# A state-space scan in three parts, three back halves copied by ScalarE, row slots inside two injections, the lag readout ahead of the scan's wait

## The chip, the core and the metric

The kernel runs on one core of a Trainium2 chip. The core has TensorE (PE; its weight loads are shown as PEld), VectorE (DVE), ScalarE (ACT), GpSimd (POOL), which here issues DMAs, and SyncE (SP), which issues the DMAs that fill a ring of weight slots. The metric is the device time of one execution in microseconds (us), and the number compared is the median of several executions.

## The reference

The kernel computes two transformer-like blocks in float32. The change touches one mixer of the second block, a diagonal state-space model with 64 groups of 16 channels and 64 complex states, run forward and backward over 256 context and 256 image tokens:

```python
def _ssm_direction(u_lat, u_ctx, a_r, a_i, bb_r, bb_i, c_r, c_i, need_ctx_out):
    ...
    hc_r, hc_i = _diag_scan(a_r, a_i, *inject(u_ctx))
    hx_r, hx_i = _diag_scan(a_r, a_i, *inject(u_lat), h0=(hc_r[-1], hc_i[-1]))
    ...
def _ssm_mixer(xn, cn, w_in, ...):
    u_x = xn @ w_in
    u_c = cn @ w_in
    ...
        y_lat = yf_x + yb_x[::-1]
    ...
        y = y.reshape(u.shape).astype(u.dtype) + d_skip * u
        val, gate = jnp.split(jax.nn.gelu(y) @ w_out, 2, axis=-1)
        return val * jax.nn.sigmoid(gate)
```

Beside it a modulation has to be ready for what follows the mixer: `silu(c) @ ada_w + ada_b`, of which three parts of 1024 columns (24 weight slots of 512 KB) are computed here.

## The kernel before

The 512 tokens are cut into 64 chunks of 8 tokens. What the tokens of a chunk give to the state at its end (the injection) comes from prepared matrices, and so do what the states give to the output (the readout) and what the tokens of a chunk give to each other's outputs (the lags, held as `TOEP`). Between them lies a scan over 64 chunk states. It stands in `XS`, 128 partitions (64 forward, 64 backward) by 64 steps by 2 (real, imaginary) by 64 groups.

**TensorE.** `turn_tokens` and `turn_groups` transpose the projected tokens. `inject(q)` (L1441) injects batch q of 8 groups with 16 matmuls of 128x128 weights and 64 columns, into PSUM at `INJ_SUMS[q]`; a float32 matmul shows as two in the profile, so 32 records. Injections 0 to 3 stand between the projection's tiles (L1467), 4 to 7 stand in a row. Then PE takes the modulation rows, `modulation()`: a generator that reads one ring slot per two steps (`row_part`, L756, two matmuls of 32 weight columns and 512 columns, four records a slot), and after eight slots waits for ScalarE's copy of the row (`row_copied`) and turns it (`turn_row`, L764). `fill(rows, 48)` advances it by 48 steps: 22 of its 24 slots and the first two turns. After that PE waits for `scanned`, and reads out (L1499 the lags, L1502 the two parts of the states, 64 and 128 matmuls, 384 records), in two halves e of 32 groups. Two transposes of the output (L1510), the last two slots (`fill(rows, 4)`), and the gated output projection `linear(8, 8, YT, ...)` (L641) follow; `fill(rows, 2)` behind its first tile turns the third row.

**VectorE** copies the back half of each injection (L2821) as it comes, in two copies of 64 partitions by 512, and scans by `within` (7 steps of a chunk of 8), `across` (6 steps) and `inner` (4 blocks), each step four dependent operations (L2780 to L2783). The groups are cut in two: `first`, 16 groups, whose scan lies between the copies, and `rest`, 48 groups, which begins when all eight injections are copied.

**ScalarE** copies the front half of each injection, then the states of the first groups into `HS` (`states`, eight copies), two modulation rows, the states of the rest (the last of them gives `scanned`), the readout's sums, the GELU, and the third row.

**Queues.** SP refills the four-slot ring: the load of slot m is issued when slot m-3 has begun to be read. POOL loads the batches, 1 MB each, behind waits: batches 0 to 7 are injection matrices, 8 to 15 readout matrices. 12, 9 and 10 wait for the seventh injection, 11 for the eighth, 13 for the landing of 11, 14 for the first inner block of `rest` (`states_ready` 5), 15 for the last (`states_ready` 8).

All orders are written out by hand; each engine executes its own list in order.

## Time and profile before

| | us |
|---|---|
| median of three executions | 3953.61 |
| lowest, highest | 3952.71, 3961.68 |
| the profiled execution | 3964.36 |
| its span, first to last instruction | 3962.6 |
| mean granted clock of TensorE in it | 0.982 of full |

The profiled execution is 10.75 us longer than the median. The stage of the change lies between about 2857 and 2972 us of its span. In a timeline a row gives start, duration, engine, line, operation, shapes, and in brackets the idle time before it and what ended it. The clock is 1.00 at 2.4 GHz and 0.50 at 1.2 GHz.

### The profile page before, as it was taken

Reading aid. Unit: us, or ns where it says so; the run is one execution under the profiler, and the core shown is the slowest. Engines: PE = TensorE matmul, PEld = TensorE weight load, DVE = VectorE, ACT = ScalarE, POOL = GpSimd, SP = SyncE. Lnnn points to the kernel's source line nnn. Section 1 sums busy time; section 2 is a strip of 40 time slices with the busy share of each in tenths; the row PEclk is TensorE's granted clock in tenths of the full one; section 3 lists DMA queues with packets and bytes.
Section 4 is the critical chain, followed back from the end, with each engine's and each line's share of the span. In section 5 each row is a group of like instructions: output and inputs, shape, how many; then the busy total and the mean of one; then the engine's idle time right before and its main releaser. Section 6 shows DMA issues by size and latency. Waiting matters only on the chain.

```text
span 3962.6 us, 61384 instructions
## 1 busy us (share of the span) xinstructions
PE 3851.4 (97%) x21346; PEld 3186.8 (80%) x21346; DVE 2844.3 (72%) x5169; ACT 1584.7 (40%) x2439; POOL 88.3 (2%) x101
## 2 busy tenths in 40 slices
PE   8999999999999999999999999999979999999998
PEld 7897799544977888888888888888748888888887
DVE  6432266894888799999897777776553997777776
ACT  5201053231228444444484444444321094444443
POOL 0000000000000000000000000000400000000000
PEclk9999999999999999999999999999969999999999
DMA  5214555475434666666615666666765516666664
GB/s 194 85 44 127 160 186 158 148 233 179 152 116 138 193 194 191 192 194 188 199 59 186 190 188 188 189 187 207 174 214 162 168 55 196 189 187 190 191 187 152
DMA packets 203773, 666.53 MB, mean 168 GB/s; under 512 B 35920, under 2 KB 46176, under 8 KB 202480
## 3 DMA queue, kind: packets, MB, share of 16 engines
q1 hardware_dynamic: 166816, 602.71, 48.6%
q0 software_dynamic: 12496, 52.53, 4.2%
q10 hardware_dynamic: 24320, 9.37, 0.9%
q8 instruction: 92, 1.51, 0.2%
q14 instruction: 49, 0.40, 0.0%
HBM read 637.34 MB, written 26.15 MB: 167 GB/s over the span
## 4 chain that ended last, share of the span: by engine, by line
PE 89%; DVE 8%; DMA 1%; ACT 1%; issue 1%; SPq 0%; DVEq 0%; ACTq 0%
PE psum L1093 27%; PE psum L1079 17%; PE psum L1081 9%; PE psum L641 6%; PE psum L701 5%; PE psum L726 4%; PE psum L1172 4%; PE psum L1267 3%; PE psum L1161 2%; DVE arena L2367 1%; PE psum L1059 1%; DMA ring<-in_w 1%; DVE arena L2368 1%; PE psum L756 1%; PE psum L1138 1%; DVE arena L2369 1%
## 5 line engine op out<-in xcount | busy, mean ns | idle before, releaser
L1093 PE MATMUL psum<-rows_split_odd,coef_split 128*128 128x512 f32 x2400 | 590.5, 396 | 3.6 <-DVE rows_split_odd L2511 3.6
L1093 PE MATMUL psum<-rows_split,coef_split 128*128 128x512 f32 x2208 | 532.1, 390 | 0.3 <-issue 0.3
L2516 DVE TENSOR_REDUCE work<-psum 128x256 f32<-128x512 f32 x360 | 249.0, 692 | 394.3 <-PE psum L1081 393.2
L1093 PEld LDWEIGHTS psum<-rows_split_odd,coef_split 128*128 128x128 f32 x2400 | 437.9, 188 | 104.9 <-issue 6.8
L1079 PE MATMUL psum<-input_split,rows_split 128*128 128x512 f32 x1440 | 514.0, 397 | 1.2 <-DVE rows_split L2511 1.2
L1079 PE MATMUL psum<-input_split,rows_split_odd 128*128 128x512 f32 x1440 | 510.0, 393 | 0.0
L1726 ACT ACTIVATE work<-work 128x256 f32<-128x256 f32 x360 | 150.7, 419 | 876.8 <-DVE work L2516 876.8
L2511 DVE TENSOR_TENSOR rows_split_odd<-ring,rows_split_odd 128x1024 fp32r<-128x1024 f32 x380 | 462.5, 1218 | 8.9 <-ACT rows_split_odd L1528 8.9
L1093 PEld LDWEIGHTS psum<-rows_split,coef_split 128*128 128x128 f32 x2208 | 401.9, 188 | 81.6 <-issue 0.9
L1528 ACT ACTIVATE rows_split_odd<-ring 128x1024 fp32r<-128x1024 f32 x380 | 400.7, 1056 | 157.5 <-PE psum L1093 154.2
L2511 DVE TENSOR_TENSOR rows_split<-ring,rows_split 128x1024 fp32r<-128x1024 f32 x364 | 442.9, 1217 | 5.3 <-ACT rows_split L1528 5.3
L1528 ACT ACTIVATE rows_split<-ring 128x1024 fp32r<-128x1024 f32 x364 | 383.6, 1054 | 126.9 <-PE psum L1093 125.6
L1081 PE MATMUL psum<-input_split,rows_split_odd 128*128 128x256 f32 x1440 | 405.2, 281 | 0.0
L1081 PE MATMUL psum<-input_split,rows_split 128*128 128x256 f32 x1440 | 403.9, 280 | 0.0
L1528 ACT ACTIVATE arena<-psum 128x1024 f32<-128x1024 f32 (+6 forms) x207 | 175.8, 854 | 385.1 <-PE psum L1267 108.5
L1079 PEld LDWEIGHTS psum<-input_split,rows_split 128*128 128x128 f32 x1440 | 270.5, 188 | 66.2 <-ACT arena L1528 1.4
L1079 PEld LDWEIGHTS psum<-input_split,rows_split_odd 128*128 128x128 f32 x1440 | 270.4, 188 | 61.8
L1081 PEld LDWEIGHTS psum<-input_split,rows_split_odd 128*128 128x128 f32 x1440 | 271.5, 189 | 8.0
L1081 PEld LDWEIGHTS psum<-input_split,rows_split 128*128 128x128 f32 x1440 | 271.6, 189 | 6.9
L641 PE MATMUL psum<-arena,ring 128*128 128x256 f32 (+1 forms) x992 | 247.4, 407 | 4.1 <-DVE arena L2267 1.3
L641 PEld LDWEIGHTS psum<-arena,ring 128*128 128x128 f32 x992 | 187.8, 190 | 56.7 <-issue 28.8
L1172 PEld LDWEIGHTS psum<-work 128*128 128x128 f32 x1536 | 182.8, 193 | 42.6 <-issue 26.6
(448 smaller groups left out, 5319.0 us busy)
## 6 DMA issues: line engine op xcount, KB each, us to landing
ring<-in_u SPq DMA_DIRECT2D x384, 512.0 KB, 3.6
ring<-in_v SPq DMA_DIRECT2D x384, 512.0 KB, 3.5
ring<-in_w SPq DMA_DIRECT2D x372, 512.0 KB, 3.7
scratch_inj<-stage ACTq DMA_DIRECT2D x16, 512.0 KB, 5.4
arena<-scratch_inj POOLq DMA_DIRECT2D x7, 1024.0 KB, 8.3
scratch_cm<-work POOLq DMA_DIRECT2D x8, 512.0 KB, 5.9
scratch_cm<-arena POOLq DMA_DIRECT2D x8, 512.0 KB, 4.9
arena<-scratch_parked POOLq DMA_DIRECT2D x4, 1024.0 KB, 8.4
```

What stands on the lines that cost most here:

```text
L641: last = mm(bank(t % 2)[0:m, 0:n], ring[:, (w0 + s // 8) % RING, (s % 8) * P:(s % 8) * P + m], rhs[:, k, 0:n], start=(k == 0), stop=(k == ...
L701: last = mm(bank(t % 2)[:, 0:S], UPR[:, t % 3, w, P * k:P * k + P], UPI[:, k, x, :], start=(k == 0 and w == 0 and x == 0), stop=(k == 7 an ...
L726: ins = mm(bank(t % 2)[:, 0:S], ring[:, (w0 + s // 8) % RING, (s % 8) * P:(s % 8) * P + P], rhs[:, k, 0:S], start=(k == 0), stop=(k == kt ...
L1079: mm(bank(b), SPL[b][:, 0, 0, P * k:P * k + P], HR[:, k, :, :], start=(k == 0), stop=False, skip_group_check=True)
L1081: last = mm(bank(b)[:, 0:S], SPL[b][:, 0, 1, P * k:P * k + P], HR[:, k, 0, :], start=False, stop=(k == 7), skip_group_check=True)
L1093: last = mm(bank(2 + 2 * i + f), CFR[:, b, c, P * i:P * i + P], parts[:, v, 512 * f:512 * f + 512], start=(first and c == 0 and v == 0), s ...
L1172: last = mm(PS(1024 * b + P * t, P), EB[:, b, t, :], EA[:, b, t, :], start=(t % 4 == 0), stop=True, skip_group_check=True)
L1267: last = mm(bank(t % 2)[:, 0:S], ring[:, L.slots % RING, k * P:k * P + P], HT[:, k, :], start=(k == 0), stop=(k == 7))
L1528: copy = lambda o, i: f(o, i, ACT.Copy)
L1726: f(AC[:, b, :], AC[:, b, :], ACT.Gelu_apprx_tanh).then_inc(sem("gelu_done"), 1)
L2511: tt(parts[:, 1, :], ring[:, w % RING, :], parts[:, 0, :].bitcast(F32), ALU.subtract)\
L2516: dve.tensor_reduce(AC[:, b, :], bank(b).rearrange("p (x t) -> p t x", x=2), AX, ALU.add)\
```

## The change

- VectorE scans in three parts: groups 0 to 15, 16 to 31 (`second`), 32 to 63 (`rest`). The first two are scanned after the back halves of injections 0 to 3 are copied, and ahead of the others.
- ScalarE copies the back halves of injections 4, 5 and 6 (`SCALAR_BACK`) ahead of the front half of each. VectorE copies 0 to 3 and 7.
- The row slots begin inside injections 5 and 6, one slot behind every two groups, so eight slots; `fill(rows, 36)` behind injection 7 takes the other sixteen and two turns. The rows use PSUM bank 7, not 4.
- The 64 lag matmuls stand ahead of the wait for `scanned`, behind all rows. The readout behind it holds the 128 matmuls of the states.
- POOL's waits for batches 14 and 15 count four inner blocks more.

```diff
+        SCALAR_BACK = (4, 5, 6)
...
-            pool.wait_ge(sem("states_ready"), 5)
+            pool.wait_ge(sem("states_ready"), 9)
...
-            pool.wait_ge(sem("states_ready"), 8)
+            pool.wait_ge(sem("states_ready"), 12)
...
-            def inject(q):
+            def inject(q, beside=iter(())):
...
+                    if g % 2:
+                        fill(beside, 2)
                 L.mark(last, "injected")
...
-            for q in range(5, 8):
-                inject(q)
+            pe.wait_ge(sem("modulation_operands"), 5)
+            rows = modulation(7)
+            for q in range(5, 7):
+                inject(q, rows)
+            inject(7)
+            fill(rows, 36)
             pe.wait_ge(sem("injected_evacuated"), 8)
             pe.wait_ge(sem("injected_back_evacuated"), 8)
-            pe.wait_ge(sem("modulation_operands"), 5)
-            rows = modulation()
-            fill(rows, 48)
+            pe.wait_ge(sem("toep_loaded"), 16 * 32)
+            for e in range(2):
+                for g in range(8):
+                    for j in range(4):
+                        q = 4 * e + j
+                        mm(PS(1024 * e + P * g, P)[NCH * j:NCH * j + NCH, :], UG[:, 8 * q + g, NCH:],
+                           TOEP[:, 8 * q + g].rearrange("p t c -> p (t c)"),
+                           start=(g % 4 == 0), stop=False, skip_group_check=True)
             L.take("scanned")
...
                 L.take("injected")
+                if q in SCALAR_BACK:
+                    for h in range(2):
+                        n = slice(NCH * h, NCH * h + NCH)
+                        last = copy(XS[B, n, :, 8 * q:8 * q + 8].rearrange("p n r g -> p g r n"),
+                                    PS(INJ_SUMS[q], 8, 2, 64)[B, :, :, n][:, :, :, ::-1])
+                    L.mark(last, "injected_back_evacuated")
...
             states(slice(0, 16))
-            for m in range(2):
-                L.take("row_ready")
-                L.give(copy(MR1, bank(4)), "row_copied")
-            L.give(states(slice(16, NG)), "scanned")
+            L.take("row_ready")
+            L.give(copy(MR1, bank(7)), "row_copied")
+            states(slice(16, 32))
+            L.take("row_ready")
+            L.give(copy(MR1, bank(7)), "row_copied")
+            L.give(states(slice(32, NG)), "scanned")
...
-            first, rest = slice(0, 16), slice(16, NG)
-            for q in range(8):
+            first, second, rest = slice(0, 16), slice(16, 32), slice(32, NG)
...
+            for q in range(4):
+                injected_back(q)
...
+            inner(first, range(4, 8))
+            within(second, range(1, 8))
+            across(second)
+            inner(second, range(4, 8))
+            for q in range(4, 8):
+                injected_back(q)
```

TensorE's list from the last injections to the readout, before. L1441 is an injection, L756 row slots (two a slot), L764 a row's turn, L1499 the lags:

```order
L1441 MATMUL psum<-arena 128x64 x16
L1419 MATMUL psum<-small,arena 128x64 x8
L1441 MATMUL psum<-arena 128x64 x32
L1441 MATMUL psum<-arena,H 128x64 x16
L756 MATMUL psum<-ring,extra 32x512 x16
L764 MATMUL psum<-tail,stage 128x2x2 x4
L756 MATMUL psum<-ring,extra 32x512 x16
L764 MATMUL psum<-tail,stage 128x2x2 x4
L756 MATMUL psum<-ring,extra 32x512 x12
L1499 MATMUL psum<-arena 32x128 x4
```

The same place in the changed kernel, from the end of injection 6. The lines are now L1442, L757, L765, L1497 for the lags and L1508 for the states:

```order
L1442 MATMUL psum<-arena 128x64 x4
L757 MATMUL psum<-ring,extra 32x512 x2
L1442 MATMUL psum<-arena 128x64 x4
L757 MATMUL psum<-ring,extra 32x512 x2
L1442 MATMUL psum<-arena,H 128x64 x16
L765 MATMUL psum<-tail,stage 128x2x2 x4
L757 MATMUL psum<-ring,extra 32x512 x16
L765 MATMUL psum<-tail,stage 128x2x2 x4
L757 MATMUL psum<-ring,extra 32x512 x16
L1497 MATMUL psum<-arena 32x128 x64
L1508 MATMUL psum<-H,arena 32x128
```

What moved: eight slots went into two injections, and the first row's turn now stands directly behind injection 7, with sixteen slots and all the lags behind it.

ScalarE's list at the same place in the changed kernel, from injection 6 on, with the semaphores it waits for. The two copies of 64x8x2x32 are a back half, 64x8x2x64 is a front half, those from `arena` are states, `stage<-psum` is a modulation row:

```order
L1535 ACTIVATE arena<-psum 64x8x2x32 [waits injected]
L1535 ACTIVATE arena<-psum 64x8x2x32
L1535 ACTIVATE arena<-psum 64x8x2x64
L1535 ACTIVATE arena<-psum 64x8x2x64 [waits injected]
L1535 ACTIVATE arena<-arena 64x18x16 [waits states_ready]
...
L1535 ACTIVATE arena<-arena 64x14x16
L1535 ACTIVATE stage<-psum 128x512 [waits row_ready]
L1535 ACTIVATE arena<-arena 64x18x16 [waits states_ready,row_copied]
```

What moved: the back halves came in; the copy of the first row stands, as before, behind injection 7's front half and the eight state copies.

TensorE's list behind the readout, before (L1510 transposes, L756 the last two slots, L641 the output projection, L764 the third row's turn):

```order
L1510 MATMUL psum<-small,arena 128x128 x16
L756 MATMUL psum<-ring,extra 32x512 x4
L641 MATMUL psum<-arena,ring 128x256 x8
L764 MATMUL psum<-tail,stage 128x2x2 x4
L641 MATMUL psum<-arena,ring 128x256 x72
```

And in the changed kernel:

```order
L1517 MATMUL psum<-small,arena 128x128 x16
L765 MATMUL psum<-tail,stage 128x2x2 x4
L642 MATMUL psum<-arena,ring 128x256 x80
L679 MATMUL psum<-arena,small 128x256
L642 MATMUL psum<-arena,ring 128x256 x8
```

What moved: the last two slots are gone from here, and the third row's turn, which waits for ScalarE's copy of that row, now stands ahead of the projection's first tile and not behind it.

## Rows read from the trace of the kernel before

**Rows 1.** The page: busy time, share of the span and instructions of each engine.

```profile
PE 3851.4 (97%) x21346; PEld 3186.8 (80%) x21346; DVE 2844.3 (72%) x5169; ACT 1584.7 (40%) x2439; POOL 88.3 (2%) x101
```

**Rows 2.** Timeline of TensorE, from injection 3 to the output projection.

```profile
2859.43 3.79 PE L1441 MATMUL psum<-arena 128*128 128x64 f32 x32
...
2871.09 13.91 PE L1441 MATMUL psum<-arena 128*128 128x64 f32 x64
2884.79 7.03 PE L1441 MATMUL psum<-arena,H 128*128 128x64 f32 x32
2893.84 3.63 PE L756 MATMUL psum<-ring,extra 128*32 128x512 f32 x12 [2.01 <-ACT arena L1528]
...
2915.64 1.87 PE L764 MATMUL psum<-tail,stage 128*128 128x4 f32 x8 [0.72 <-ACT stage L1528]
...
2919.56 1.92 PE L756 MATMUL psum<-ring,extra 128*32 128x512 f32 x4 [0.17 <-DMA ring<-in_w]
...
2931.80 1.05 PE L756 MATMUL psum<-ring,extra 128*32 128x512 f32 x4 [1.64 <-DMA ring<-in_w]
...
2948.94 0.64 PE L1499 MATMUL psum<-arena 128*32 128x128 f32 x4
...
2962.39 1.97 PE L1510 MATMUL psum<-small,arena 128*128 128x128 f32 x16
...
2966.44 3.69 PE L641 MATMUL psum<-arena,ring 128*128 128x256 f32 x16 [1.08 <-issue]
2969.97 0.95 PE L764 MATMUL psum<-tail,stage 128*128 128x4 f32 x8
```

**Rows 3.** Windows: busy us of each engine, granted clock, DMA share, GB/s.

```profile
2866.00:2868.00 2.00, 2.00 (x20) 2.00 (x20) 1.86 (x6) 0.50 (x2) 0.14 (x1) 1.00 0.98 352
2872.00:2892.00 20.00, 19.83 (x93) 19.64 (x93) 6.98 (x14) 4.42 (x5) 2.63 (x3) 0.50 0.39 126
2892.00:2929.00 37.00, 22.16 (x66) 4.51 (x68) 35.51 (x57) 5.45 (x10) 1.77 (x2) 0.50 0.80 273
2930.00:2939.00 9.00, 3.70 (x22) 1.40 (x20) 8.76 (x11) 5.74 (x7) 0.89 (x1) 1.00 0.92 327
```

**Rows 4.** Groups of VectorE by shape, 2826 to 2942: busy us, mean ns.

```profile
L2821 DVE COPY arena<-psum 64x512 f32<-64x512 f32 x16 | 15.2, 1022 | 55.5 <-PE psum L1441 55.5
L2780 DVE TENSOR_TENSOR work<-work,arena 128x768 f32<-128x768 f32 x7 | 6.7, 958 | 0.3
L2780 DVE TENSOR_TENSOR work<-work,arena 128x256 f32<-128x256 f32 x7 | 3.0, 426 | 0.3
L2780 DVE TENSOR_TENSOR work<-work,arena 128x96 f32<-128x96 f32 x6 | 1.5, 258 | 0.2
L2780 DVE TENSOR_TENSOR work<-work,arena 128x32 f32<-128x32 f32 x6 | 1.2, 192 | 0.2
```

**Rows 5.** Timeline of VectorE: the back half of injection 3; rest's first operation.

```profile
2863.32 1.89 DVE L2821 COPY arena<-psum 64x512 f32<-64x512 f32 x2 [2.13 <-PE psum L1441]
...
2893.84 0.96 DVE L2780 TENSOR_TENSOR work<-work,arena 128x768 f32<-128x768 f32 x1
```

**Rows 6.** Timeline of ScalarE: last front half, states, rows, GELU.

```profile
2891.86 1.87 ACT L1528 ACTIVATE arena<-psum 64x1024 f32<-64x1024 f32 x1 [4.94 <-PE psum L1441]
2893.55 3.38 ACT L1528 ACTIVATE arena<-arena 64x288 f32<-64x288 f32 x8
...
2966.85 1.06 ACT L2014 ACTIVATE arena<-arena 128x1024 f32<-128x1024 f32 x1 [0.51 <-DVE arena L2849]
2967.81 0.58 ACT L1528 ACTIVATE stage<-psum 128x512 f32<-128x512 f32 x1
```

**Rows 7.** The chain of waits; a DMA piece runs from issue to landing.

```profile
2933.02 7.66 DMA ring<-in_w
```

**Rows 8.** Timeline of POOL: the issue of batch 15.

```profile
2941.09 0.88 POOL L485 DMA_DIRECT2D work<-scratch_cm  x1 [9.45 <-DVE arena L2783]
```

**Rows 9.** DMA issues around batch 14's: KB, us from issue to landing.

```profile
arena<-scratch_cm POOLq DMA_DIRECT2D x1, 1024.0 KB, 8.6
```

More of the change, by code:

```diff
@@ L1029, in _, with modulation @@
             keep_busy(4, 1)
-            def modulation():
+            def modulation(b=4):
                 for m in range(3):
@@ L1036, in modulation @@
                         for f in range(2):
-                            last = row_part(4, L.slots, k, f)
+                            last = row_part(b, L.slots, k, f)
                             if f == 0:
@@ L1480, in _ @@
             turn_groups(7)
-            for q in range(5, 8):
-                inject(q)
+            pe.wait_ge(sem("modulation_operands"), 5)
[4 more added lines that the diff above has]
+            fill(rows, 36)
             pe.wait_ge(sem("injected_evacuated"), 8)
             pe.wait_ge(sem("injected_back_evacuated"), 8)
-            pe.wait_ge(sem("modulation_operands"), 5)
-            rows = modulation()
-            fill(rows, 48)
+            pe.wait_ge(sem("toep_loaded"), 16 * 32)
[6 more added lines that the diff above has]
+                           start=(g % 4 == 0), stop=False, skip_group_check=True)
             L.take("scanned")
-            pe.wait_ge(sem("toep_loaded"), 16 * 32)
             for e in range(2):
@@ L1493, in _ @@
                 for g in range(8):
-                    for part in range(3):
+                    for part in range(2):
                         for j in range(4):
                             q = 4 * e + j
-                            o = PS(1024 * e + P * g, P)[NCH * j:NCH * j + NCH, :]
-                            if part == 0:
-                                mm(o, UG[:, 8 * q + g, NCH:], TOEP[:, 8 * q + g].rearrange("p t c -> p (t c)"),
-                                   start=(g % 4 == 0), stop=False, skip_group_check=True)
-                            else:
-                                last = mm(o, HS[:, :, part - 1, 8 * q + g], BATCHES[8 + q][0][:, g, part - 1, :],
-                                          start=False, stop=(part == 2), skip_group_check=True)
+                            last = mm(PS(1024 * e + P * g, P)[NCH * j:NCH * j + NCH, :],
+                                      HS[:, :, part, 8 * q + g], BATCHES[8 + q][0][:, g, part, :],
+                                      start=False, stop=(part == 1), skip_group_check=True)
                     if g % 4 == 3:
@@ L2015, in _ @@
             L.take("row_ready")
-            L.give(copy(MR1, bank(4)), "row_copied")
+            L.give(copy(MR1, bank(7)), "row_copied")
             evacuate(8, lambda t, ps: f(SG[:, t, :], ps[:, 0:S], ACT.Sigmoid))
@@ L2814, in inner, with injected_back @@
                                    ST1[:, 0:7, :, g], ST2[:, 0:7, :, g]), "states_ready")
-            first, rest = slice(0, 16), slice(16, NG)
-            for q in range(8):
+            first, second, rest = slice(0, 16), slice(16, 32), slice(32, NG)
+            def injected_back(q):
                 L.take("injected")
+                if q in SCALAR_BACK:
+                    return
                 for h in range(2):
@@ L2830, in _ @@
                     across(first)
-                if q == 3:
-                    inner(first, (4, 5))
-                if q in (4, 5):
-                    inner(first, (q + 2,))
+            dve.wait_ge(sem("injected_back_evacuated"), 4)
+            dve.wait_ge(sem("injected_evacuated"), 4)
+            inner(first, range(4, 8))
[4 more added lines that the diff above has]
+                injected_back(q)
             dve.wait_ge(sem("injected_back_evacuated"), 8)
```

## The prediction

> **What bounds the kernel now.** The page first [rows 1]: TensorE is busy for 97% of the span, VectorE for 72%, so as a rule only TensorE's own work or its waits move the end. The stage of this change is the exception. In the timeline of TensorE [rows 2] injection 7 ends at 2891.8 (2884.79 and 7.03), and from there to the readout's begin at 2948.94 PE does nothing but modulation rows, with waits for their slots between them; in the windows it is busy for 22.2 of 37 us and for 3.7 of 9 us [rows 3]. VectorE scans the last 48 groups in the same time, from 2893.84 on [rows 5], and is done at about 2941, when POOL issues batch 15 behind the last inner block [rows 8]. So two chains run beside each other: the scan, done at 2941 and copied soon after, and the rows, whose last slot begins at 2948.6. **The rows are the later by some 6 us.** The readout starts behind both and takes 13.1 us (2948.94 to 2962.0, where L1510 can start).
>
> What limits the rows is the ring. From slot 10, begun at 2919.56, to slot 15, begun at 2931.80, five slots take 12.24 us: 2.45 us a slot [rows 2], though a slot is 0.9 to 1.7 us of PE. The next load is issued only when an earlier slot has been begun, and a batch in between costs extra: the slot load of 2933.02 took 7.66 us [rows 7] where batch 14 (8.6 us [rows 9]) lay ahead of it. At the 273 GB/s of the window from 2892 [rows 3] a batch of 1.05 MB is 3.8 us of the queues.
>
> **The clock.** In this execution PE's clock is 1.00 up to 2868 and 0.50 in the window from 2872 to 2892 [rows 3]; before it fell, PE had left the projection's wide matmuls and did transposes and 64-column injections. An injection costs 3.79 us at 2.4 GHz and 7.03 at 1.2 GHz [rows 2]. Three injections make 3 x 3.24 = 9.7 us. The median lies 10.75 us below the profiled execution, so I take it that at least half of the executions keep the full clock here, and work the change out for both.
>
> **The change, part by part.**
>
> *VectorE's split.* Four operations of a step take 4 x 0.426 at 256 elements and 4 x 0.958 at 768 [rows 4]; by the line between them 512 elements take 0.692, 448 take 0.625 and, from the short shapes (0.192 at 32, 0.258 at 96), 64 take 0.225. The last part is then 7 x 2.77 + 6 x 0.90 + 4 x 2.50 = 34.8 us where the old one lasted 47 (2893.84 to 2941): 12 us less behind the last copy. The second part costs 7 x 1.70 + 6 x 0.77 + 4 x 1.57 = 23 us, and lies behind the back half of injection 3 (2865.2 [rows 5]) and four inner blocks of the first part (6.3 us): VectorE is free at 2894.5.
>
> *ScalarE's back halves.* VectorE loses three pairs of 1.0 us copies, ScalarE gains as much: 3.9 us an injection and not 1.87 [rows 6]. With slots in between, an injection lasts longer than that, so it hides, but for what stands behind injection 7.
>
> *Slots inside injections.* Four slots each in injections 5 and 6. A slot alone is 1.7 us at half clock (1.92 of the record at 2919.56 less its tail), 0.9 at full. They run while the DMA share is low (0.39 between 2872 and 2892 [rows 3]), which is the gain: eight slots are off the ring's back early. The price is on PE's own list: injection 7 ends 8 x 1.7 = 13.7 us later at half clock, at 2905.5, and at full clock 8 x 0.9 = 7 us later plus about 2 us for slot 3, which is only asked for when slot 0 has begun. Who waits for that is VectorE: its last part starts at 2907.5 in the first case, so that the scan ends at 2942.3, **one us later than now**; the 12 us are spent. At full clock PE is 9.7 us earlier in both kernels; there the last part starts when VectorE is free and has copied injection 7, at 2896.4, and the scan ends at 2931.2, as it would before (2941 - 9.7).
>
> *A new wait.* Row 0 is now complete inside injection 6, but ScalarE copies it only behind injection 7's front half (1.87), eight state copies (3.38) and the copy itself (0.6) [rows 6]. PE stands at the turn for 1.9 + 3.4 + 0.6 = 5.9 us behind injection 7, with sixteen slots queued behind it and three of them loaded. Before, this wait was 0.72 us [rows 2]. The turn is 1.87 us at half clock, 0.95 at full. So the sixteen slots start at 2913.4 at half clock and at about 2897 at full clock. Three are there at once; thirteen must come through the ring, together with batches 11, 13 and 14.
> - Full clock: I estimate the first six reloads for 2913 (three asked for from 2898 on, batch 13 behind them, three more behind it); seven more at 2.45 make 2930.2, batch 14 adds 3.8, the last slot 1.7: the rows end at 2935.7.
> - Half clock: the first reload is asked for at about 2915, behind batch 13, and with the 5 to 7 us of such loads is there at about 2921; twelve at 2.45 make 2950.4, batch 14 adds 3.8 and the last slot 1.7: 2955.9. If the slots come at 2.0 us it is 2950.5.
>
> *Lags ahead of the wait.* 64 of 192 matmuls, a third of 13.1 us, would come off the path if PE stood idle before `scanned`. By the sums above it doesn't: the rows end after the scan in both cases, so lags and states together still take 13.1 us behind them. Saved: 0, up to 4.4 where the scan is the later.
>
> Readout's end: full clock 2935.7 + 13.1 = 2948.8 where the old one would be 2962.0 - 9.7 = 2952.3, **3.5 us less**; half clock 2955.9 + 13.1 = 2969.0 against 2962.0, **7.0 us more** (1.6 more at 2.0 us a slot).
>
> *Behind the readout.* The third row's turn moves ahead of the projection's first tile. It waits for ScalarE's row copy, which stands behind both GELU halves and ends at 2968.4 [rows 6]; with the turn of 0.95 the first tile starts at 2969.3 and ends at 2973.0, where before it and the turn ended at 2970.9 [rows 2]: **2.0 us more**. The two slots that are gone lay in a wait: 0. PE now idles for 4 us there; should the clock fall, a stretch of the projection costs up to 1.7 us more.
>
> *The rest.* Bank 7 for bank 4, POOL's counts: 0. Batch 15 is issued at the scan's end and lands some 6 us later, before the second half of the readout needs it.
>
> **The sum.** On the profiled execution with its clock: 3964.4 + 7.0 + 2.0 = 3973.4 (3968 to 3975). With the full clock in the injections, which is how I read the median: 3953.6 - 3.5 + 2.0 = 3952.1, and with the clock's risk behind the readout 3953, my forecast.
>
> The Trainium skill, "DMA: Bandwidth & Descriptors", section "Issuing engines are not separate DMA queues", has DMAs of all issuers interleave on the same 16 engines. The row differs: the slot load of 2933.02 landed at 2940.68, behind a batch issued 2.3 us earlier, as if queued. By the page a slot would share and land some 2 us sooner, and the sum would be 3951; the row decides.
>
> **The rivals.**
> - *The rows keep up, the scan sets the end.* The readout then starts at the scan's end plus under 2 us of copies, 2933 at full clock, with the lags done, and needs 13.1 x 2/3 = 8.7 us, less at full clock throughout: 2941 against 2952.3, less 11, plus 2.0: 3945. For it: eight slots ahead. Against it: the new wait and 2.45 us a slot. Chance 0.15.
> - *The rows end late, at half clock*: slower. It decides where PE's clock has fallen before injection 5. Eight slots at 1.7 us then hold injection 7 back by 13.7 us, VectorE idles from 2894.5, and the sum above gives 3973.4 on the profiled execution; as a median 3962 to 3974, the likeliest 3968. For it: two of four executions lie at 3962 or above. Chance 0.27.
> - *The slots lift the clock.* From 2930 the clock is back at 1.00, after row slots that followed one another closely [rows 3]. Dense slots between injections could do the same, and injections and slots after it would take half. By the sums this is the full-clock case a few us late: 3953 to 3957 where the clock would have fallen, and where scan and rows both gain, 3940. The Trainium skill, "TensorE: Matmul & The Clock Gate", section "What's actually happening", has activity release a throttled default, which speaks for it; but in the windows from 2892 to 2929 the slots ran at 0.50 [rows 3]. Chance 0.08, half of it at 3940.
> - The forecast's own case holds 0.5, between 3946 and 3961.
>
> **How the numbers follow.** About 0.3% of 3953.6 is 11.9 us, what a measurement can tell from no change. Faster by more (under 3941.7): half of the third rival and a little of the first, 0.08. Slower by more (above 3965.5): most of the second, 0.22. Same: 0.70. The range takes in the first rival's 3945 with a margin and the second up to its end: 3943 to 3972.
>
> **What the profile after would show.** Slots between injection passes of two groups, about 13.8 us an injection at 0.50 or 7.2 at 1.00; PE idle for about 6 us behind injection 7, ended by ScalarE's copy into `stage`; the last part of the scan near 35 us; sixteen slots in 36 to 43 us; lags straight behind the last slot, and no long wait for `scanned`; the first projection tile behind the turn. I am wrong if PE waits for `scanned` behind the lags for several us (first rival), if the row copy comes at once, or if the slots come at PE's own pace.

## The result, and the profile after

The changed kernel takes 3972.74 us in the median of 17 executions, the kernel before 3962.05 in 17: a ratio of 1.0023, with a 95% interval from 1.0014 to 1.0033, so slower by about 9 us. The forecast was 3953, with a range from 3943 to 3972. (One execution of the changed kernel, at 5216.73 us with a mean clock of 0.69, is left out of the ratio.) The three executions of the kernel before that I had seen, median 3953.61, were low ones as a set: the kernel before was timed again beside each group of experiments, with medians of 3962.72 (31 executions), 3962.79 (30) and 3962.72 (32), and with the 17 above all its 110 executions lie between 3947.40 and 3971.16.

The page after shows nothing of this at its first level, as [rows 1] did not:

```profile
PE 3866.0 (97%) x21346; PEld 3193.5 (80%) x21346; DVE 2848.9 (72%) x5231; ACT 1592.1 (40%) x2453; POOL 88.2 (2%) x101
```

TensorE's timeline of the changed kernel, from injection 3 to the projection, answers [rows 2] (start, duration, engine, line, operation; in brackets the idle time before and what ended it):

```profile
2863.00 3.79 PE L1442 MATMUL psum<-arena 128*128 128x64 f32 x32
...
2875.08 1.97 PE L1442 MATMUL psum<-arena 128*128 128x64 f32 x8
2876.97 1.92 PE L757 MATMUL psum<-ring,extra 128*32 128x512 f32 x4
...
2905.10 7.09 PE L1442 MATMUL psum<-arena,H 128*128 128x64 f32 x32
2917.95 1.87 PE L765 MATMUL psum<-tail,stage 128*128 128x4 f32 x8 [5.76 <-ACT stage L1535]
2919.76 3.63 PE L757 MATMUL psum<-ring,extra 128*32 128x512 f32 x12
2927.95 1.92 PE L757 MATMUL psum<-ring,extra 128*32 128x512 f32 x4 [4.56 <-DMA ring<-in_w]
...
2958.33 1.06 PE L757 MATMUL psum<-ring,extra 128*32 128x512 f32 x2 [3.01 <-DMA ring<-in_w]
...
2972.21 1.97 PE L1517 MATMUL psum<-small,arena 128*128 128x128 f32 x16
2978.26 1.87 PE L765 MATMUL psum<-tail,stage 128*128 128x4 f32 x8 [4.08 <-ACT stage L1535]
2979.99 10.31 PE L642 MATMUL psum<-arena,ring 128*128 128x256 f32 x38
```

A quarter of an injection and a slot alternate from 2875.08 on, 3.75 us a pair, so injections 5 and 6 last 15.0 us each; injection 7 ends at 2912.2. Then PE stands for 5.76 us for ScalarE's row copy, as forecast, sixteen slots take until 2960.2, and a second wait of 4.08 us is new behind the readout. The windows, in the columns of [rows 3], show the clock:

```profile
2872.00:2892.00 20.00, 20.00 (x76) 12.52 (x75) 18.45 (x61) 7.85 (x7) 0.00 (x0) 0.50 0.60 191
2892.00:2932.00 40.00, 29.46 (x103) 15.92 (x104) 24.77 (x44) 12.87 (x22) 4.40 (x5) 0.50 0.72 240
...
2977.00:2983.00 6.00, 4.74 (x15) 4.20 (x16) 0.35 (x2) 1.21 (x2) 0.00 (x0) 0.50 0.13 16
```

The clock is 0.50 in the injections, though PE is busy for every one of the 20 us from 2872. It is also 0.50 where the projection begins, where the kernel before had 1.00 [rows 2: the turn took 0.95, here 1.87].

ScalarE's timeline (against [rows 6]) is what the two new waits stand behind: the front half of injection 7, eight copies of states, then the row; and at the end, the row behind both GELU halves.

```profile
2912.23 1.87 ACT L1535 ACTIVATE arena<-psum 64x1024 f32<-64x1024 f32 x1 [5.03 <-PE psum L1442]
2913.91 3.38 ACT L1535 ACTIVATE arena<-arena 64x288 f32<-64x288 f32 x8
2917.30 0.60 ACT L1535 ACTIVATE stage<-psum 128x512 f32<-128x512 f32 x1
...
2977.63 0.58 ACT L1535 ACTIVATE stage<-psum 128x512 f32<-128x512 f32 x1
```

VectorE's groups of 2862 to 2952 (busy us, mean ns; against [rows 4]) and the issue of batch 15 at the scan's end (against [rows 8]):

```profile
L2795 DVE TENSOR_TENSOR work<-work,arena 128x512 f32<-128x512 f32 x7 | 4.8, 692 | 0.2
L2795 DVE TENSOR_TENSOR work<-work,arena 128x448 f32<-128x448 f32 x4 | 2.5, 625 | 0.1
```

```profile
2949.45 0.88 POOL L486 DMA_DIRECT2D work<-scratch_cm  x1 [6.64 <-DVE arena L2798]
```

Steps of 692 and 625 ns are those of the forecast. The chain of waits (start, duration, what) names what holds the rows, three loads of the ring where [rows 7] had one such:

```profile
2922.71 7.33 DMA ring<-in_w
...
2943.14 7.65 DMA ring<-in_w
...
2952.93 5.36 DMA ring<-in_w
```

**One ruler for all kernels.** The table counts from the start of injection 3, ahead of which all code is the same. Everything behind the start of the next stage takes 929.5 to 929.7 us in all fourteen profiles, so in a profiled execution the column "next stage" carries the whole effect of an edit, while injection 3 itself starts anywhere from 2851.6 to 2865.9 us. The scan's end is the issue of batch 15, the last slot is the last one ahead of the readout, and the readout's end is the start of the transposes behind it. These columns come from one profile of each kernel. The medians come from 9 to 17 executions of it (for the kernel before, from the 32 beside the last experiments), the ratios are to the kernel before as timed beside the same group, with 95% intervals. Column and median don't always move by the same amount: b1 is 10.4 us shorter in the stage and 4.0 in the median, a2 gains 6.4 us of the stage on the changed kernel and 1.4 in the median.

| kernel | inj. 7 ends | scan ends | last slot begins | readout ends | next stage | median us | ratio |
|---|---|---|---|---|---|---|---|
| before | 32.4 | 81.7 | 89.2 | 103.0 | 173.5 | 3962.7 | |
| changed | 49.2 | 86.5 | 95.3 | 109.2 | 184.5 | 3972.7 | 1.0023 (1.0014 to 1.0033) |
| a1, last two slots back | 48.9 | 86.2 | 88.5 | 102.2 | 172.7 | 3968.0 | 1.0013 (1.0003 to 1.0023) |
| a2, row copy first | 49.1 | 86.5 | 89.1 | 103.8 | 178.1 | 3971.3 | 1.0015 (1.0004 to 1.0026) |
| a3, no slots inside | 33.2 | 72.4 | 94.3 | 106.1 | 180.4 | 3971.6 | 1.0023 (1.0013 to 1.0032) |
| b1, before with wide matmuls | 22.2 | 71.5 | 79.2 | 92.6 | 163.1 | 3958.7 | 0.9983 (0.9973 to 0.9993) |
| c1, changed, all mended | 31.8 | 72.3 | 67.0 | 84.5 | 155.0 | 3944.9 | 0.9967 (0.9954 to 0.9980) |
| c2, b1 with three slots later | 22.2 | 71.5 | 70.4 | 86.7 | 163.3 | 3954.9 | 0.9984 (0.9972 to 0.9995) |
| c3, changed with wide matmuls | 31.8 | 72.3 | 82.1 | 95.5 | 170.5 | 3955.6 | 0.9987 (0.9973 to 1.0001) |
| c4, before with lags ahead | 33.0 | 82.3 | 86.1 | 99.7 | 170.3 | 3958.6 | 0.9996 (0.9981 to 1.0011) |
| d1, c1, slots behind | 23.0 | 72.3 | 74.7 | 88.4 | 159.0 | 3952.0 | 0.9979 (0.9967 to 0.9991) |
| d2, c1, lags behind the wait | 31.7 | 72.3 | 68.0 | 86.5 | 157.0 | 3947.1 | 0.9963 (0.9952 to 0.9974) |
| d3, c1, scan in two parts | 31.9 | 81.3 | 67.9 | 91.9 | 162.5 | 3954.0 | 0.9980 (0.9971 to 0.9988) |
| d4, c1 without wide matmuls | 49.3 | 86.6 | 81.7 | 98.2 | 168.7 | 3959.7 | 0.9984 (0.9970 to 0.9998) |

From before to changed the stage grows by 11.0 us: 6.2 up to the readout's end and 4.8 behind it. The other 3.5 us between the two profiled spans (3962.6 and 3977.1) lie ahead of injection 3, where nothing was changed. What goes with it in the traces is the clock: summed over the stretch ahead of injection 3, it is at 0.50 for 37 us in the profile with the earliest start (c3) and for 75 us in the one with the latest (a2).

### The profile page after: what moved, and what is told of

Read it like the earlier page. It is cut to its first block, busy times and chain, and to the rows that moved or that the text cites. A ratio compares the mean times of both kernels' runs of the same rounds, so it can differ in the third digit from the quotient of the medians.

```text
span 3977.1 us, 61458 instructions
## 1 busy us (share of the span) xinstructions
PE 3866.0 (97%) x21346; PEld 3193.5 (80%) x21346; DVE 2848.9 (72%) x5231; ACT 1592.1 (40%) x2453; POOL 88.2 (2%) x101
## 4 chain that ended last, share of the span: by engine, by line
PE 89%; DVE 8%; ACT 1%; DMA 1%; issue 1%; SPq 0%; DVEq 0%; ACTq 0%
PE psum L1094 27%; PE psum L1080 17%; PE psum L1082 9%; PE psum L642 6%; PE psum L702 5%; PE psum L1173 4%; PE psum L727 4%; PE psum L1268 3%; PE psum L1162 2%; PE psum L757 2%; DVE arena L2382 1%; PE psum L1060 1%; DVE arena L2383 1%; PE psum L1139 1%; DVE arena L2384 1%; PE psum L1442 1%
## 5 line engine op out<-in xcount | busy, mean ns | idle before, releaser
L1535 ACT ACTIVATE arena<-psum 128x1024 f32<-128x1024 f32 (+7 forms) x213 | 182.0, 862 | 395.3 <-PE psum L1268 108.5
```

Of the source, the lines that this page charges most:

```text
L1535: copy = lambda o, i: f(o, i, ACT.Copy)
```

## The experiments

**a1: the last two slots back behind the readout's transposes.**

```diff
-            fill(rows, 36)
+            fill(rows, 32)
```

> The changed kernel, but behind injection 7 only 32 steps of the rows are taken and not 36, so that the last two slots and the third row's turn stand behind the readout as in the kernel before. Theory A (the turn ahead of the projection's first tile costs PE a wait of 6 us at a clock that falls): from the readout's end to the projection's second tile 8.4 to 8.6 us as before, where the changed kernel took 13.2; the time 4 to 6 us under the changed kernel's, so about 3967. The rows ahead of the readout also end 2 to 4 us sooner (two slots fewer). Rival B (the tail is hidden behind GELU and costs nothing): the time within 1 us of the changed kernel's.

The readout ends 7.0 us earlier and the stretch behind it is the old one (70.5 us to the next stage, 75.3 in the changed kernel): 11.8 us of the stage hang on these two slots and the third row's turn, which the edit moves together. The time is 3968.0 (about 3967 expected), and the rows end 6.8 us sooner, where 2 to 4 were expected. Behind the readout PE now has work instead of the wait, in a1's timeline:

```profile
2966.94 1.06 PE L757 MATMUL psum<-ring,extra 128*32 128x512 f32 x8
2969.09 3.69 PE L642 MATMUL psum<-arena,ring 128*128 128x256 f32 x16 [1.08 <-issue]
```

The tile takes 3.69 us, so the clock did not fall there. In the profile a1 is 0.8 us shorter in the stage than the kernel before, but its median is 5.3 us above. The profiled span is longer too, by 2.6 us, with injection 3 starting 3.4 us later; why the median is above stays open.

**a2: ScalarE copies row 0 ahead of its front half of injection 7.**

```diff
-            for q in range(5, 8):
+            for q in range(5, 7):
                 injected(q)
+            L.take("row_ready")
+            L.give(copy(MR1, bank(7)), "row_copied")
+            injected(7)
...
             states(slice(0, 16))
-            L.take("row_ready")
-            L.give(copy(MR1, bank(7)), "row_copied")
```

> The changed kernel, but ScalarE copies the first row ahead of injection 7's front half, not behind it and eight state copies. Theory A (PE's 5.8 us wait for this copy holds sixteen slots back): the wait behind injection 7 shrinks from 5.8 us to under 1, the first slot behind it starts 5 us sooner, and the readout ends 3 to 5 us sooner; time about 3968. Rival B (the ring and its batches set the rate of the slots, whenever PE is ready): the wait goes, but the last slot begins within 1.5 us of where it was, and the time stays at 3971 to 3974.

The wait of 5.76 us is gone, in a2's timeline:

```profile
2914.81 1.81 PE L765 MATMUL psum<-tail,stage 128*128 128x4 f32 x8
2916.56 3.63 PE L757 MATMUL psum<-ring,extra 128*32 128x512 f32 x12
```

The last slot begins 6.2 us earlier and the readout ends 5.4 earlier: the new wait went fully into the rows. With all 24 slots ahead of the readout this only just makes up for the two that were moved. In the stage this is theory A (3 to 5 us expected at the readout); the median, 3971.3, moved by 1.4 us only, within the noise and where rival B had it, so the gain of a2 alone rests on its profile.

**a3: no slots inside the injections, all 24 behind injection 7.**

```diff
-            for q in range(5, 7):
-                inject(q, rows)
-            inject(7)
-            fill(rows, 36)
+            for q in range(5, 8):
+                inject(q)
+            fill(rows, 52)
```

> The changed kernel, but no slots inside the injections: all 24 stand behind injection 7. Theory A (eight slots at 1.85 us hold VectorE's last part back by 14 us): injection 7 ends at 32 us behind injection 3's start (changed kernel 49), the scan's last part starts at about 35 and ends at 71 to 73 (changed kernel 86). The rows, 24 slots through the ring, end at 106 to 112 behind injection 3's start, later than the changed kernel's 97, and lags and states behind them: readout's end 119 to 124 where the changed kernel has 109. Time 3982 to 3988. Rival B (the slots inside are what makes it slow): the readout ends before 107, time under 3968.

Here I had expected the rows to end 10 us or more later. They end a microsecond earlier (94.3 against 95.3), and the readout 3.1 earlier. Eight slots taken off the ring early bought nothing at this clock, since injection 7 came 16 us later for them and a wait of 5.76 us with them. The run mixes the two, as the wait goes too. It also shows the scan by itself: batch 15 is issued at 2927.34, 72.4 behind injection 3, so three parts, with ScalarE's share of the copies, end the scan 9.3 us earlier than two, and the rows hide all of it. POOL's timeline, then TensorE's, of a3:

```profile
2927.34 0.88 POOL L486 DMA_DIRECT2D work<-scratch_cm  x1 [6.65 <-DVE arena L2797]
```

```profile
2949.22 0.62 PE L757 MATMUL psum<-ring,extra 128*32 128x512 f32 x2 [0.79 <-DMA ring<-in_w]
```

**b1: the kernel before with two matmuls of 128x512 (an existing helper, results unused) ahead of injection 4.**

```diff
             turn_groups(6)
+            keep_busy(2, 7)
             inject(4)
```

> The kernel before with two wide matmuls (128x512, into an unused bank) ahead of injection 4. Theory A (the clock falls in this stage in most executions, because of the narrow work and the wait ahead of injection 4): with them the clock stays at 1.00 through injections 5 to 7, these take 11.5 us and not 21, and the time is 7 to 10 us under the kernel before, about 3953, which is also what its two fastest executions have. Rival B (the fall has nothing to do with this stage's order, or the injections are hidden): the time within 2 us of the kernel before's 3962.

TensorE's timeline and windows of b1:

```profile
2867.22 1.99 PE L685 MATMUL psum<-small 128*128 128x512 f32 x4
2869.04 3.68 PE L1441 MATMUL psum<-arena 128*128 128x64 f32 x32
...
2873.30 7.36 PE L1441 MATMUL psum<-arena 128*128 128x64 f32 x64
```

```profile
2868.00:2883.00 15.00, 15.00 (x130) 14.20 (x128) 11.45 (x22) 7.25 (x6) 2.76 (x4) 1.00 0.67 214
```

The clock holds through injection 7. Injections 5 and 6 take 7.36 us, where [rows 2] had 13.91, and the readout ends 10.4 us earlier. This is the forecast's case of a full clock in the injections, which no profile shows without these matmuls. In the seven profiles without the wide matmuls the clock fell 7.7 to 8.6 us behind injection 3's start, in the seven with them it held until injection 7 was over. Whether it is the width of these matmuls or the 2 us that they add no run tells apart. The time was expected near 3953, 7 to 10 us under the kernel before; it is 3958.7, 4.0 under, with an interval that reaches from 3 to 11 us.

**c3: the changed kernel with the same two matmuls.**

```diff
             turn_groups(6)
+            keep_busy(2, 7)
             inject(4)
```

> The changed kernel with two wide matmuls (128x512, into an unused bank) ahead of injection 4. Theory A (at half clock the eight slots inside the injections hold injection 7 back by 15 us and the wait for ScalarE's copy comes on top; at full clock the injections and slots take half): the clock stays at 1.00 through injection 7, which ends at 32 to 34 us behind injection 3's start (changed kernel 49.2); the scan ends at 72 to 74 (86.2), the readout at 97 to 101 (109.2); from injection 3's start to the next stage 172 to 177 where the changed kernel took 184.5; time 3961 to 3966. Rival B (the clock makes no difference because the rows come at the ring's rate anyway): the readout ends within 3 us of 109.

Against b1, at the same clock, the change costs 2.9 us up to the readout's end (95.5 against 92.6) and 4.5 behind it: the next stage begins 7.4 us later. The forecast had it 3.5 earlier and 2.0 later. So even on its own premise the working was off by some 6 us at the readout, and it is the rows again: the last slot begins at 82.1, where b1 has 79.2. The new wait is there at this clock too, and the clock fell in it, so that the turn behind it took 1.87 us, in c3's timeline:

```profile
2889.19 1.87 PE L765 MATMUL psum<-tail,stage 128*128 128x4 f32 x8 [5.76 <-ACT stage L1536]
```

Against what was expected of c3 the readout is earlier (95.5, not 97 to 101), and so are the next stage (170.5, not 172 to 177) and the time (3955.6, not 3961 to 3966).

**c1: the changed kernel with a1's, a2's and c3's edits together.**

```diff
             turn_groups(6)
+            keep_busy(2, 7)
...
-            fill(rows, 36)
+            fill(rows, 32)
...
-                injected(q)
+            L.take("row_ready")
+            L.give(copy(MR1, bank(7)), "row_copied")
+            injected(7)
```

> The changed kernel with its three suspected losses mended at once: two wide matmuls ahead of injection 4, the first row copied ahead of injection 7's front half, and two slots and the third row's turn left behind the readout. Theory A (these three are all that keeps the change's slots, split and lags from paying): the slots ahead of the readout end at 73 to 77 us behind injection 3's start, near the scan's end, the readout at 84 to 90, the stage takes 154 to 160, time 3948 to 3954, at least 4 us under the kernel before with the wide matmuls alone (3958.7). Rival B (the idea itself doesn't pay: the slots taken early come out of injection time and the ring's rate decides): 3957 to 3961, no better than the wide matmuls alone.

The best version: 3944.87 us (3948 to 3954 expected), 0.9967 of the kernel before, 18.5 us less in the stage. The last slot begins at 67.0 (an end at 73 to 77 was expected), ahead of the scan's end, and what ends the chain is a batch. In c1's chain of waits:

```profile
2935.27 6.65 DMA work<-scratch_cm
...
2942.06 5.39 PE psum L1509 x128
```

Batch 15, issued when the scan ends, lands 6.65 us later, and the second half of the readout stands behind it.

**c2: b1 with three more slots behind the readout.**

```diff
-            fill(rows, 48)
+            fill(rows, 42)
...
-            fill(rows, 4)
+            fill(rows, 10)
             linear(8, 8, YT, ...
```

> The kernel before with the two wide matmuls, and five slots behind the readout, not two (19 ahead of it, not 22). Theory A (the rows through the ring, 2.4 us a slot, are what the readout waits for): three slots fewer ahead end the rows 7 us sooner, at 73 behind injection 3's start (80 with the wide matmuls alone), with the scan's copy at 73; the readout ends at 86 to 88 (92.6). Behind it five slots cost up to 5 us more than two. Stage 159 to 163 (163.1), time 3954 to 3959. Rival B (the scan is the later of the two): the readout's end moves by less than 2 us.

The readout ends 5.9 us earlier than in b1 (86.7, with 86 to 88 expected), the next stage begins at the same time. Five slots don't fit behind the readout; c2's timeline there:

```profile
2951.48 1.91 PE L756 MATMUL psum<-ring,extra 128*32 128x512 f32 x12
2956.20 3.19 PE L756 MATMUL psum<-ring,extra 128*32 128x512 f32 x8 [2.81 <-DMA ring<-in_w]
2959.32 4.08 PE L641 MATMUL psum<-arena,ring 128*128 128x256 f32 x16
```

So slots can't simply be pushed to the other side; two fit there, without cost.

**c4: the kernel before with the lags ahead of the wait, alone** (the rows in bank 7).

```diff
             fill(rows, 48)
-            L.take("scanned")
+            for e in range(2):
+                for g in range(8):
+                    for j in range(4):
+                        mm(..., TOEP[:, 8 * q + g]...)
+            L.take("scanned")
```

> The kernel before with one part of the change alone: the 64 lag matmuls ahead of the wait for the scan, and the rows in bank 7. Theory A (the rows end after the scan, so nothing of the lags is hidden): readout's end at 103 us behind injection 3's start within 1.5 us, time within 2 us of the kernel before's 3962. Rival B (PE waits for the scan and the lags fill that wait): readout's end 3 to 4.4 us sooner, time 3958.

By the readout's end and the time alone this looks like rival B: 3.3 us earlier, 3958.6. The slots say otherwise. The last one begins 3.1 us earlier than in the kernel before (86.1 against 89.2), and from there the readout takes 13.6 us where it took 13.8. So in this profile the lags ahead of the wait saved some 0.2 us, as theory A has it, and the rest came from the rows, which are not what the edit changes. Why the rows ended earlier is open; the clock came back after 30.7 us here, where it stayed down for 61.4 in the kernel before. The ratio's interval includes 1.

**d1, d2, d3: c1 with one part undone each.** d1 has ScalarE's row copy where the change has it, since the row is complete later; d2 has the readout of the kernel before; d3 has its lists of VectorE and ScalarE for the scan.

```diff
 d1
-            for q in range(5, 7):
-                inject(q, rows)
-            inject(7)
-            fill(rows, 32)
+            for q in range(5, 8):
+                inject(q)
+            fill(rows, 48)
 d2
-                    for part in range(2):
+                    for part in range(3):
 d3
-            first, second, rest = slice(0, 16), slice(16, 32), slice(32, NG)
+            first, rest = slice(0, 16), slice(16, NG)
```

> The changed kernel with two wide matmuls of 128x512 ahead of injection 4, no slots inside the injections and 22 slots behind injection 7: the best version so far (3944.9 us) without its slots inside, to tell what these are worth where the clock is full. Theory A, the slots inside pay there: the rows then come from the ring as in the kernel before with the wide matmuls (last slot 79.2 us behind injection 3's start, where the best version has 67.0), lags and states come behind them, the readout's end is near 93 (84.5 in the best version) and the time 3953 to 3958. Rival B, they win nothing, as in the run at half clock where they were put behind (95.2 against 96.2): last slot at 67 to 70, readout's end at 84 to 87, time 3945 to 3948.

> The best version so far with the lag matmuls put back behind the wait for the scan. Theory A, the states' matmuls wait for batch 15 anyway (it is issued at the scan's end, 72.3, and landed at 79.0 in the best version, and the second half needs it): the lags then fill part of that wait, the readout's end moves from 84.5 to about 86.3 and the time by 1.8, to 3946 to 3947.5. Rival B, the lags are all on the path: 4.4 us more, the readout's end at 88.9 and 3949.3.

> The best version so far with the scan in two parts again (16 and 48 groups), VectorE copying all back halves. Theory A, the three parts are worth what they take off the last one (about 12 us) less what injection 7 comes later: the last part of 47 us starts about a microsecond behind injection 7 (31.8), the scan ends near 80.8, batch 15 lands near 87.3, the readout ends at 91 to 93 (84.5 in the best version) and the time is 3951 to 3954. Rival B, the rows set the end in both: readout's end at 84 to 86, 3944 to 3946.

Readout's end against c1's 84.5: d3 91.9 (91 to 93 expected), d1 88.4 (between the 93 and the 84 to 87 of the two theories), d2 86.5 (86.3 expected). So with the clock held in the injections and the rows out of the way the three parts, with ScalarE's copies, are worth 7.4 us, the slots inside 3.9 and the lags 2.0. The lags are worth less than a third of the readout because in c1 half of what they save goes into a wait for batch 15 between the readout's halves. TensorE's timeline of c1, the start of each half:

```profile
2936.22 0.33 PE L1509 MATMUL psum<-H,arena 128*32 128x128 f32 x1 [1.79 <-ACT arena L1536]
2942.06 0.30 PE L1509 MATMUL psum<-X,arena 128*32 128x128 f32 x1 [2.11 <-DMA work<-scratch_cm]
```

In d2 PE stands for 3.62 us before the first half, with no lags to fill that wait, but the lags of the first half then run while batch 15 is on its way, and the second half starts without the 2.11 us. That is theory A of d2. The times are 3954.0 for d3 (3951 to 3954 expected), 3952.0 for d1 (just under theory A's 3953 to 3958) and 3947.1 for d2 (3946 to 3947.5 expected).

The ratios of c1 and d2 overlap (0.9967 and 0.9963): the lags' 2.0 us is read from the profiles and not shown by the times. The intervals of d1 and d3 touch c1's as well, though their medians are 7 and 9 us above it.

**d4: c1 without the wide matmuls**, that is, the changed kernel with a1's and a2's edits.

```diff
             turn_groups(6)
-            keep_busy(2, 7)
```

> The changed kernel with the row's copy ahead of ScalarE's front half of injection 7 and the last two slots back behind the readout's transposes, but without the wide matmuls, so with the clock as it is. Theory A, the two mends add up: the last slot ahead of the readout begins near 85, ahead of the scan's end at 86.2; batch 15 lands near 93 and the readout ends at 97 to 99 (103.0 in the kernel before, 102.2 with the slots alone mended), time 3956 to 3960. Rival B, without the clock the ring takes back what the copy gives: readout's end at 102, 3964 to 3968.

The readout ends at 98.2 (97 to 99 expected), the median is 3959.7 (3956 to 3960 expected), 0.9984 of before. At the low clock the mended change wins 4.8 us in the stage, and the end hangs on the scan and batch 15 again, in d4's chain:

```profile
2946.91 7.80 DMA work<-scratch_cm
```

## Why the prediction was wrong

**The step that failed is the choice of the clock.** "The median lies 10.75 us below the profiled execution, so I take it that at least half of the executions keep the full clock here." In none of the seven profiles without the wide matmuls does it hold. The 10.75 us were a sample of three: the profiled execution (3964.36) is near the median of the later groups (3962.7 to 3962.8), and over the fourteen profiles the start of injection 3 alone varies by 14 us. A difference between one execution and a median of three was put down to the first place that could hold it. So the forecast of 3953 missed 3972.7 in two pieces: some 9 us because its base, 3953.6, was no median of the kernel before, and the rest because the change costs some 10 us where 1.5 less was worked out. The other sum, on the profiled execution with its clock, was 3973.4; the median is 3972.7. It was the second rival, with a chance of 0.27.

A smaller share of the executions may well keep the clock. The fastest of d4 took 3938.54 us, 20 less than all but one of the others, at a mean clock of 0.991, which leaves about 71 us at 0.50 in the whole execution; d4's profile has 68 in the stage alone, and no profile has under 37 ahead of it. By this estimate the clock was not down in that stage for as long as the profile shows. Of the kernel before, 13 of 110 executions took under 3954 us. None of these was profiled, so this is argued and not shown.

The terms of that other sum, at half clock, predicted and measured:
- *Injection 7 later*: 13.7 and 16.8 us. A slot between two pieces of an injection costs 1.85 us and not 1.7 (8 x 0.15 = 1.2), injection 4 ended later by 0.4, and the pieces of injection at 1.9 add the rest (8 x 1.90 = 15.2 for what the kernel before did in 13.7).
- *The scan ends*: one us later and 4.8. The last part took about what was worked out (its steps measure 692 and 625 ns); it is injection 7's lateness, 3.1 us more than worked out, that came through.
- *A new wait*: 5.9 and 5.76. Right.
- *Ring*: sixteen slots from 2919.76, the last at 2958.3, 2.57 us a slot; 2.45 predicted. The last slot is over at 2960.2 where 2955.9 was worked out, but in this execution injection 3 stood 3.6 us later: behind injection 3 both are the same within a microsecond. That is in part luck. The first reload was worked out for 61.6 behind injection 3 and landed at 64.9, and the twelve behind it, with batch 14, took 30.4 us where 33.2 was worked out; the two errors cancel.
- *Lags ahead of the wait*: 0 saved. Right: the scan and its copies were done at 87.4 behind injection 3, PE was not at the wait by then.
- *Readout's end*: 7.0 later and 6.2. Right in size, again with luck: the sum adds 1.7 us for the last slot and then 13.1 for the readout, which in [rows 2] begins 0.3 us behind that slot's start. From the last slot's start to the readout's end it was 13.9 us, and not 14.8.
- *Behind the readout*: 2.0 and 4.8. The wait was foreseen (4 us of idle; 4.08); its price was mis-sized. The clock fell to 0.50 in it: the turn took 1.87 instead of 0.95, and the first tile 1.7 more. The text had this as a risk of up to 1.7; it belongs in the sum.

None of the signs named for being wrong came, and most of what the profile after was to show did (the wait of 6 us, the last part of 35, sixteen slots in 40.5): the list holds for the half-clock case as well, so it could not tell the forecast from its second rival, but for the length of injections 5 and 6.

**The full-clock working was off as well.** c3 against b1 is the change with the clock held in the injections: +7.4 us to the next stage, where the text had -1.5. The working put the start of the sixteen slots at 2897, which is 37.6 behind injection 3, and left out the turn ahead of them; c3 has 39.4, with a turn of 1.87 us at the clock that had fallen. It put the sixth reload at 2913, which is 53.6; in c3 it landed at 59.3, since the first loads behind the wait took 7.3 to 7.9 us and the next three 5.9 to 6.5. The seven behind it and batch 14 took 22.8 us, 21.0 worked out. So the mis-sized term is the first six reloads, 16 us for what took 19.9. The forecast's "same" thus came from a premise that was wrong and a sum that would have missed on it.

**Of the cause**, a1, a2 and d4 show what made the change slow. It is neither the scan nor the clock in the injections, which was low before too, but two placements: the last two slots ahead of the readout, with the third row's turn (11.8 us of the stage, a1), and the row's copy behind ScalarE's front half and states (6.4 us of the stage, a2). Undone together they give 15.8 us (d4), less than the sum of the two. Each of them alone is read from one profile; the two together are clear in the times, 0.9970 to 0.9998 for d4 and 1.0014 to 1.0033 for the changed kernel. Without them the same change is 4.8 us shorter in the stage than the kernel before (d4), and 8.1 us shorter with the clock held in the injections (c1 against b1). What the last two slots and the turn cost separately was not tried.

The text's reading that a slot load queues behind the batch was not put to a test. That batch 13, issued 58.2 behind injection 3, landed at 66.6, and slot loads issued at 58.8, 59.7 and 60.6 at 64.9, 67.0 and 68.3: the first of them overtook the batch, so "queued" is too strong.

## What to carry to other kernels

When two chains run beside each other and one is the later, an edit to the earlier one shows nothing until the later is cut: look first for the piece of the later chain that has a place elsewhere at no cost, as the last two slots had in a wait behind the readout. A copy that releases a producer belongs at the front of the copying engine's list, ahead of copies that nobody waits for. And a median of three executions against one profile says nothing of what happened in a stage; compare stages from a fixed point inside the trace, over several profiles.

## What the runs showed of the hardware

- PE was busy for all of the 20 us from 2872 to 2892 of the changed kernel, with injections and row slots, and the granted clock stayed at 0.50 throughout, after PE had left the projection's wide matmuls. With two 128x512 matmuls, 1.99 us, ahead of injection 4 it stayed at 1.00 through the same work (c1's windows, in the columns of [rows 3]):

```profile
2868.00:2888.00 20.00, 19.55 (x130) 12.82 (x130) 18.70 (x51) 10.08 (x10) 1.65 (x2) 1.00 0.88 279
2888.00:2896.00 8.00, 8.00 (x62) 5.98 (x64) 7.25 (x31) 5.49 (x5) 3.51 (x4) 1.00 0.89 282
```

- The Trainium skill, "TensorE: Matmul & The Clock Gate", section "What's actually happening", has activity release a throttled default. By that the 20 busy us would have come at 1.00, and the third rival with them; the changed kernel's window from 2872 to 2892, fully busy and at 0.50, differs from it, and it decides.
- Behind an idle stretch of 4.08 us the projection started at 0.50, in the changed kernel, a2, a3 and c3 alike; from the readout's end to the next stage they take 3.8 to 4.8 us more than the kernel before, the wait included. With two slots in its place (a1, c1, d1 to d4) it starts at 1.00.
- A 512 KB slot load takes 3.4 to 3.6 us where nothing else is in flight, as between the injections of the changed kernel. Three loads issued close together behind batch 13 (1 MB) took 6.1, 7.3 and 7.7 us there, and 3.6, 7.5 and 8.1 in a1. From the first slot behind injection 7 to the last ahead of the readout the ring gives one per 2.57 us in the changed kernel, 2.62 in b1 and 2.85 in c3 ((82.1 - 39.4) / 15). A slot is 0.9 to 1.9 us of PE, and the long waits between slots end with a load.
